# Another order in a convolution layer, halves in retention and the last norm, and unread products in three gaps

## The reference

```python
def conformer_conv_mixer(xn, ...):
    h = xn @ pw1_w + pw1_b
    a, gate = jnp.split(h, 2, axis=-1)
    h = a * jax.nn.sigmoid(gate)
    h = causal_depthwise_conv(h, dw_w, taps=31) + dw_b   # per feature, over the tokens
    h = layer_norm(h, ln_w, ln_b)                        # over the 1024 features
    return jax.nn.silu(h) @ pw2_w + pw2_b

def retention_mixer(xn, ...):                            # 4 heads
    q, k, v, g = split(xn @ w_in)                        # 1024, 1024, 2048, 2048 wide
    q, k = rotary(rms_norm(q)), rotary(rms_norm(k)) * dk ** -0.5
    y = group_norm(retention_chunkwise(q, k, v))
    return (jax.nn.silu(g) * y) @ w_out

out = rms_norm(x, g_final)                               # the very last step
```

## Time and profile before

| what | value |
|---|---|
| median of 3 runs | 2360.89 us (2360.59 to 2361.51) |
| the profiled execution | 2362.6 us |
| its span, first to last instruction | 2360.8 us |
| PE busy | 2311.3 us (98%) |
| DVE, ACT, POOL busy | 67%, 51%, 4% of the span |
| mean granted TensorE clock | 0.996 |

### The profile page before, as it was taken

The page is one execution under the profiler, slowest core; times in us unless marked ns, Lnnn a source line. Parts: engine busy times, 40 slices in busy tenths (PEclk is TensorE's granted clock), DMA queues, the critical chain, the costliest instruction groups (busy, mean ns, idle before and its releaser), DMA issues.

```text
span 2360.8 us, 31036 instructions
## 1 busy us (share of the span) xinstructions
PE 2311.3 (98%) x12362; PEld 1933.3 (82%) x12362; DVE 1571.2 (67%) x1650; ACT 1211.9 (51%) x1347; POOL 86.1 (4%) x136
## 2 busy tenths in 40 slices
PE   8999999889999999999999999999999999999998
PEld 6788888678888788877788877888888887888887
DVE  7666676766567765686576567867655667677555
ACT  5545445354356644464454365544644656446444
POOL 0000030200000000000000000000000000000000
PEclk9999999999999999999999999999999999999999
DMA  7454654634443355545454544445454544454543
GB/s 272 185 173 178 246 201 191 203 112 188 187 179 155 139 199 213 196 161 191 183 201 178 189 176 176 168 161 200 180 196 178 216 178 173 161 192 182 197 174 128
DMA packets 71848, 434.21 MB, mean 184 GB/s; under 512 B 11648, under 2 KB 11968, under 8 KB 26176
## 3 DMA queue, kind: packets, MB, share of 16 engines
q1 hardware_dynamic: 59184, 399.78, 44.2%
q0 software_dynamic: 12560, 32.96, 4.5%
HBM read 430.73 MB, written 6.16 MB: 185 GB/s over the span
## 4 chain that ended last, share of the span: by engine, by line
PE 93%; DVE 4%; ACT 2%; issue 1%; DMA 0%; POOL 0%; DVEq 0%; ACTq 0%
PE pair L807 21%; PE pair L810 11%; PE acc L778 10%; PE acc L779 10%; PE acc L780 10%; PE pair L778 6%; PE pair L780 5%; PE pair L779 5%; PE pair L819 4%; PE pair L820 2%; PE pair L1029 1%; DVE work L2304 1%; DVE w_lo L1926 1%; PE pair L848 1%; PE acc L1206 1%
## 5 line engine op out<-in xcount | busy, mean ns | idle before, releaser
L1926 DVE TENSOR_TENSOR w_lo<-raw,w_hi 128x2048 fp32r<-128x2048 f32 (+1 forms) x402 | 865.0, 2173 | 112.4 <-ACT w_hi L1327 108.6
L1327 ACT ACTIVATE w_hi<-raw 128x2048 fp32r<-128x2048 f32 (+1 forms) x402 | 717.0, 1805 | 53.7 <-PE acc L780 47.9
L807 PE MATMUL pair<-act,w_hi 128*128 128x512 f32 x1920 | 602.7, 395 | 0.0
L810 PEld LDWEIGHTS pair<-act,w_lo 128*128 128x128 f32 x1920 | 360.6, 188 | 84.8
L810 PE MATMUL pair<-act,w_lo 128*128 128x256 f32 x1920 | 377.3, 278 | 0.0
L778 PE MATMUL acc<-w_hi,hid 128*128 128x512 f32 x848 | 333.9, 394 | 0.0
L779 PE MATMUL acc<-w_lo,hid 128*128 128x512 f32 x848 | 330.4, 390 | 0.0
L780 PE MATMUL acc<-w_hi,hid 128*128 128x512 f32 x848 | 330.2, 389 | 0.0
L807 PEld LDWEIGHTS pair<-act,w_hi 128*128 128x128 f32 x1920 | 295.5, 189 | 3.6
L1472 ACT ACTIVATE gate<-pair 128x512 f32<-128x512 f32 x104 | 62.2, 598 | 458.2 <-PE pair L810 435.8
L2116 DVE TENSOR_TENSOR gate<-pair,gate 128x512 f32<-128x512 f32 x104 | 71.7, 690 | 255.0 <-ACT gate L1472 254.6
(11 more groups left out here) (273 smaller groups left out, 2671.9 us busy)
## 6 DMA issues: line engine op xcount, KB each, us to landing
raw<-weights SPq DMA_DIRECT2D x354, 1024.0 KB, 6.7
raw<-weights SPq DMA_DIRECT2D x52, 512.0 KB, 4.0
work<-bias_scratch POOLq DMA_DIRECT2D x32, 192.0 KB, 2.7
val<-gains POOLq DMA_DIRECT2D x11, 512.0 KB, 4.0
bias_scratch<-bias_rows POOLq DMA_DIRECT2D x4, 1024.0 KB, 19.9
hid<-u_rows POOLq DMA_DIRECT2D x20, 142.0 KB, 3.4
work<-ret_gn_w POOLq DMA_DIRECT2D x8, 256.0 KB, 5.3
work<-ret_gn_b POOLq DMA_DIRECT2D x8, 256.0 KB, 5.8
```

The lines of the kernel that those rows point to most:

```text
L807: mm(tiles(o[:, 512 * n:512 * n + 512]), h[:, k, n * P:(n + 1) * P], both[:, :, k, :], start=k == 0, stop=False)
L810: last = mm(o[:, 512 * n:512 * n + SEQ], l[:, k, n * P:(n + 1) * P], both[:, 0, k, :], start=False, stop=k == KT - 1)
L1327: run(w_hi[slot][:, part], raw[slot][:, part], ACT.Copy).then_inc(hi_done, 1)
L1926: tt(w_lo[slot][:, part], raw[slot][:, part], w_hi[slot][:, part].bitcast(F32), ALU.subtract).then_inc(lo_done, 1)
```

## The change

1. **Conformer, DVE's order.** `gated(1)` moves from tap 14 to tap 6, the split of unit 35 from tap 15 to 9, `gated(2)` from 27 to 14, `gated(3)` from behind the loop to tap 28 and without the split of unit 36, which comes after the loop.
2. **Conformer, the rough mean.** It is taken from tiles 2 and 3 (PE's) and no longer from tiles 0 and 1 (DVE's). PE convolves tiles 2, 3, 4, then makes the rough mean, then tiles 5, 6, 7. ACT copies tiles 2 to 4 out of PSUM with their bias; DVE takes the rough mean off tiles 0 to 4 in one instruction (128x1280) and ACT squares these five in one. The last products become four from six: tile 6 is added on DVE. `C_DSQ` is made before `C_DELTA`. POOL waits for a pair to be read, and no longer for a square, before it overwrites a place `C_X`.
3. **Retention by halves.** PE signals `token_half` after tokens 0 to 127 of a q, k or v unit; ACT copies (and squares) that half then, and the other at the unit's end. The roots come before `rotate_evac`.
4. **The last norm by halves.** DVE scales columns 0 to 511, ACT columns 512 to 1023, and SP stores four blocks of 128x512; POOL stores nothing.
5. **Unread products.** `keep_busy` issues float32 matmuls of 128x128 by 128 columns whose result nobody reads: 18 on zeroes before anything has been loaded, 12 after the first turned half at the start, 24 before unit 36 in the Conformer layer.

```diff
+            def keep_busy(m, n):
+                for _ in range(n):
+                    mm(IDLE, m, m, start=True, stop=True)
...
+            pe.wait_ge(warm_in, 1)
+            keep_busy(WARM, 18)
             pe.wait_ge(loaded, 16)
             first_half()
+            keep_busy(ident[:], 12)
...
                 unit_f()
                 unit_f()
-                pe.wait_ge(conv_ready, 2)
+                uses = [convolve(n) for n in range(3)]
+                assert uses[0] == CONV_PAIR
+                await_drained(uses[1])
                 o = open_pair()
-                for k in range(2):
-                    last = mm(o[:, 0:SEQ], C_MEAN, C_Y[:, k, :], start=k == 0, stop=k == 1)
+                for k in (2, 3):
+                    last = mm(o[:, 0:SEQ], C_MEAN, C_Y[:, k, :], start=k == 2, stop=k == 3)
                 last.then_inc(pair_full, 1)
-                uses = [convolve(n) for n in range(len(STACKED_TILES))]
+                uses += [convolve(n) for n in range(3, 6)]
                 o = open_pair()
                 pe.wait_ge(summed, 1)
...
-                for k in (6, 7):
-                    await_drained(uses[k - 2])
...
+                await_drained(uses[5])
+                mm(o[:, 0:SEQ], C_MEAN, C_Y[:, 7, :], start=False, stop=True).then_inc(mean_ready, 1)
+                pe.wait_ge(squared, 4)
+                mm(o[:, 512:512 + SEQ], C_MEAN, C_SQ[:, 7, :], start=False, stop=True).then_inc(pair_full, 1)
+                keep_busy(ident[:], 24)
...
                         if n >= 4:
-                            pool.wait_ge(squared, n - 2)
+                            p = CONV_PAIR + n - 4
+                            pool.wait_ge(drained[p % 2], p // 2 + 1)
...
-                convolve(0, 1, {4: second_piece, 14: lambda: gated(1), 15: lambda: ahead(CONV_FIRST + 3),
-                                27: lambda: gated(2)})
-                gated(3)
-                use(False)
+                convolve(0, 1, {4: second_piece, 6: lambda: gated(1), 9: lambda: ahead(CONV_FIRST + 3),
+                                14: lambda: gated(2), 28: lambda: gated(3)})
+                ahead(CONV_FIRST + 4)
+                for _ in range(4):
+                    use(False)
+                await_drained(S.p - 2)
                 await_drained(S.p - 1)
...
+                five_y = C_Y[:, 0:5, :]
+                tt(five_y, five_y, C_NEG.unsqueeze(1).broadcast_to([P, 5, SEQ]), ALU.add).then_inc(centred, 1)
...
                 for i in range(4):
-                    next_unit()
+                    ahead(S.u + 1)
                     o, done, slot = use()
-                    run(xs[:, i % 2, :], o[:], ACT.Copy).then_inc(done, 1)
...
+                    for a in range(2):
+                        if a == 0:
+                            await_half()
+                            link(run(xs[:, i % 2, wide(a)], o[:, wide(a)], ACT.Copy))
+                        else:
+                            unit_end()
+                            run(xs[:, i % 2, wide(a)], o[:, wide(a)], ACT.Copy).then_inc(done, 1)
...
+                    roots(4)
                     if i:
                         rotate_evac(i - 1)
-                    roots(4)
...
+            for a in range(2):
+                for n in range(2):
+                    sp.wait_ge(out_ready[n], a + 1)
+                    sp.dma_start(out[P * a:P * (a + 1), wide(n)], xs[:, a, wide(n)]).then_inc(out_stored, 16)
```

More of the change, by code:

```diff
@@ L389, in build_program @@
         first_copied = sem("first_copied")
+        token_half = sem("token_half")
+        out_ready = [sem(f"out_ready{n}") for n in range(2)]
+        out_stored = sem("out_stored")
+        last_root = sem("last_root")
         taps_ready = sem("taps_ready")
@@ L824, in unit_both, with unit_t @@
                 S.u += 1
-            def unit_t(middle=None, quarters=None):
+            def unit_t(middle=None, quarters=None, by_half=False):
                 o = open_pair()
@@ L882, in first_unit @@
                                      k == 0, k == KT - 1)
+                        if by_half and (a, k) == (0, KT - 1):
+                            last.then_inc(token_half, 1)
                         if a == 0 and k in (turn_at, turn_at + 1):
@@ L990, in retention @@
                         v_use = S.p
-                        unit_t(quarters=last_turn if h == 0 else None)
+                        unit_t(quarters=last_turn if h == 0 else None, by_half=True)
                     if h == 0:
@@ L1550, in retention @@
[L1550 to L1553, removed]
-                                   accum_out=ss[:, g:g + 1])
+                    for a in range(2):
[5 more added lines that the diff above has]
+                            run(xs[:, i % 2, wide(a)], o[:, wide(a)], ACT.Copy).then_inc(done, 1)
+                            await_drained(S.p - 1)
+                        for g in (2 * a, 2 * a + 1):
+                            cs = slice(SEQ * g, SEQ * (g + 1))
+                            last = run(gate[:, slot, cs], xs[:, i % 2, cs], ACT.Square, scale=RET_DK ** -0.5,
+                                       accum_out=ss[:, g:g + 1])
@@ L1564, in retention @@
                             rotate_evac(3)
-                            S.u += 1
-                            act.wait_ge(piece_used, 2 * S.u)
-                        else:
-                            next_unit()
-                            o, done, _ = use()
-                        run(R_V[:, h % 2, :, :], o[:].rearrange("p (a d) -> p a d", a=2), ACT.Copy).then_inc(done, 1)
+                        unit_end()
+                        run(R_V[:, h % 2, 1, :], o[:, wide(1)], ACT.Copy).then_inc(done, 1)
@@ L1621, in conformer @@
                 gate_unit(3, o, done)
+                for k in (2, 3, 4):
+                    o, done, _ = use(False)
+                    await_pair()
+                    run(C_Y[:, k, :], o[:, 0:SEQ], ACT.Identity, bias=colv("dw_b", k)).then_inc(done, 1)
                 o, done, _ = use(False)
@@ L1626, in conformer @@
                 act.wait_ge(centred, 1)
[L1627 to L1628 removed]
+                square(0, 5)
+                for k in (5, 6, 7):
                     use(False)
@@ L1910, in _ @@
                 square(a, 1)
-                root(a).then_inc(rstd_ready, 1)
-                S.due("x_ready")
+                root(a).then_inc(last_root, 1)
+                act.wait_ge(last_root, a + 1)
+                run(xs[:, a, wide(1)], xs[:, a, wide(1)], ACT.Copy, scale=rstd[:, a:a + 1]).then_inc(out_ready[1], 1)
             assert S.u == n_units and S.split == n_units
```

84 lines of the change are left out of this document (42 added, 42 removed).

## The result

The changed kernel takes 2349.55 us (median of 5 runs, 2348.77 to 2351.76) where the kernel before takes 2361.51 in the same comparison: a ratio of 0.9946, 95% interval 0.9933 to 0.9960. Run again in a later comparison it gave 2349.47 and 0.9945 (0.9932 to 0.9959). The forecast was 2340.0 with a range of 2335.5 to 2348.0. So the sign was right, the gain is 12 to 13 us and not 21, and the time lies just outside the range. The profiled execution took 2348.81 us with a span of 2347.0, 13.8 less than before.

The account below looks back on a forecast made before the run. PE was taken as the bound, busy 2311.3 of 2360.8 us. Gains of 13.75 (Conformer), 1.5 (unit 36), 3.5 (retention), 0.8 (start) and 1.25 (end) sum to 20.8, giving 2340.0 us, range 2335.5 to 2348.

Parts of the forecast that it names:

- (d): Conformer layer, stop of 4.29 us before tile 6: goes if loads come in time; gain 4.3, and 1.6 more.
- (a): Conformer layer: split of unit 35 comes 2.4 us or more earlier, so PE's unit ends at 443.85; gain 0.85.
- (c): Conformer layer, first four stacked tiles: 13.8 us without the lower clock, 14.8 before; gain 1.0.
- (f): Conformer closing chain up to unit 36: `C_DSQ` before `C_DELTA` starts the root some 0.3 us earlier; gain 0.15.
- Rival 1: Conformer layer, u_rows transfers still come late; 2344 to 2348, or about 2353 at worst; chance 0.17.
- middle case: Late u_rows transfers in the Conformer layer: a stop of 3 to 6 us at one tile and the clock; 2344 to 2348.
- (b): Conformer layer: tile 2 starts at the unit's end, rough mean after tile 4 at full rate, 0.9 us; gain 4.9.
- (e): Conformer closing sums: four products, no tile 6 sum at the end; 0.86 us to the same product, 1.8 before; gain 0.95.
- rival 3: DVE is the bound in the Conformer closing stage, 2 to 4 us later than counted: 2341 to 2343; chance 0.10.
- 24 unread products: Before unit 36: 5.2 us in the idle stretch, unit 36 then at full rate; net gain 1.5, bounds 0 and 2.9.
- The start: Unread products (18 and 12) around PE's first turn bring full rate earlier; gain 0.8, bounds -1.7 and 1.0.
- The end: Last norm: earlier scaling 0.35, no POOL issue delay 0.3, smaller last block 0.6; gain 1.25, bounds 0.5 and 2.

Follow-up runs that it names:

- experiment 1: Changed kernel with SP holding unit 38's load until the shifted copies of tile 7 have landed: 2342.8 us, ratio 0.9915.
- experiment 6: Changed kernel without the three calls of `keep_busy`, so without any of the 54 unread products: 2350.79 us, ratio 0.9948.

## Why the forecast missed

**The step that failed is (d).** It said that the third store and its loads run "when SP has no weight transfer in flight". Three things in it were off. First, its own rebuild had the split of unit 36 end at 454.1 and the eight loads be issued up to 455.4 and land by 459; the split's end is what lets SP load unit 38, so that load stood in the text at 454.1, in the middle of the loads. Shown: with that one load held, the stop is 1.19 and not 6.00 us (experiment 1). Second, the split of unit 35 was costed as DVE's work that comes earlier, (a), and its effect on SP only against the second store, as "5 us at 426 GB/s, done by 438". It shares the engines with eight loads of 142 KB, and the DMA engines stay busy until about 442. So the second set starts at 443.91 and POOL, which goes through its program in order, can only issue the third store at 448.27, 3 us later than forecast once the 2.0 of the earlier layers is taken off. Third, the usual landing of 3.5 us was taken from stores and loads that lay clear of the weights, while the same row's 9.9 was the price for those that don't.

What it cost: unit 36 was forecast at 473.6, 471.6 once the 2.0 us of the earlier layers are taken off, and came at 481.25. Of these 9.7 us, 7.1 are the two stops and 1.8 the clock behind the longer one; of the remaining 0.8 most is in the tiles (2 to 5 take 14.4 us without the stop, where (c) had 13.8), and 0.1 or 0.2 each in the rough mean, tiles 6 and 7, and the sums ahead of tile 7's. The closing chain held: from tile 7's product at 474.02 to unit 36 it is 7.23 us, 7.38 before, as (f) had it. With unit 38's load held the layer gives 10.0 of the 13.75 (four profiles of the old order have 85.4 on average to unit 36, this one 75.4), and 2.6 of what is then missing are its two stops.

**Rival 1 is what happened**, with 0.17 of the chances. Its middle case was a stop of 3 to 6 us; there were 6.0 and 1.06, and the time came out 1.6 us above what that case gave.

**The other steps.** (a) and (b) held: tile 2 starts at 441.75, forecast 443.85 less 2.0, and the rough mean took 1.13 and not 0.9. (c) held as to the clock: it is granted in full at tile 4, in spite of the stop ahead of it. (e) held: two products, 0.97 us, lie ahead of tile 7's, where I had counted 0.86. DVE was not the bound (rival 3): it waits 8.84 us for tile 6. Of the 24 unread products the duration was right, 5.52 us for 48 instructions is 0.23 for a product (forecast 0.215); the gain, forecast at 1.5, is 1.4 by one pair of profiles and 2.2 over all, within the bounds. Retention was forecast from the list of waits at 3.5; both layers gave 4.3, within the bounds; the 0.8 beyond the waits I haven't traced.

**The start** was forecast at 0.8; the ledger's 0.1 is the luck of one execution, and over all profiles it gave about 1 (experiment 6), so nothing shows that this step failed. The profile on which the forecast rests has its second turned half at 17.20, where the other five without products have it at 17.86 to 18.48. The overrun of 18 products was larger than "up to 1 us" in the changed kernel: the first turn starts at 8.04 for 6.79, but at 7.04 when the same program ran again. The prediction took 3.1 and 5.8 us as agreement with a half rate that differs from run to run at a start; those were two stops of one execution, and only the starts of several profiles, listed below, show it.

**The end** was forecast at 1.25 and gave 2.9. The term that was mis-sized is POOL's tail. I had counted the delay of its issue and the bytes; what follows the last byte, 2.8 us for POOL and 0.85 for SP, was in the row of the span's end and I hadn't read it. That is 2.0 of the 2.6 us from the last scaling on. The kernel with only this part ends 0.85 us after its last bytes too (moved until 2355.65, span 2356.5), and the one with only retention, which keeps POOL's store, 2.8 (2354.2, 2357.0). The Trainium skill, DMA: Bandwidth & Descriptors (Anatomy of one DMA — SWDGE (gpsimd) path), puts most of some 2 us of fixed cost of GpSimd's path behind the last byte. The profile agrees in kind: in the layer, too, the DMA engines have all but fallen idle at 442.5 (a share of 0.05 from there to 443), and POOL, which waits for the second store, goes on at 443.91. Of SP's path no figure stands there. Of the same page's first byte after 0.6 us (Specifications) the measurement is 0.86, from the issue at 2343.91 to the first bytes at about 2344.77.

**What stays open.** The best kernel here is the changed one with unit 38's load held, 2342.8 us, 6.8 below the changed kernel where both ran side by side (2349.47 and 2342.67, with 12 products). It still has stops of 1.43 and 1.19, since the second store is waited for 10.35 us. An order in which units 37 and 38 both miss all of POOL's transfers wasn't found: the three places tried for unit 37 each met one of them. Why the parts' product is 0.0012 below the whole I can't say; the intervals allow for nothing at all.

## What to carry to other kernels

A split or a buffer release that moves earlier takes its refill (the load into the buffer that it frees) with it: write down for each queue when its transfers are now in flight, and lay them beside all others in order of time, before any of them is given its usual landing. A transfer of 142 or 287 KB that met a 2 MB load took 7 to 10 us here and not 3 to 4; making the big load wait was worth 6.8 us, and here a load that had slack was better held than hurried. Follow PE past the stop that is taken away to the next engine's work: at the start 2.4 us between PE's first products were 0.4 one unit later. And read a gain of 1 us in more than one pair of profiles: two single executions put the start at 0.1 and unit 36 at 1.4, and fourteen put them at about 1 and at 2.2.

## What the runs showed of the hardware

- DMA engines can be fully busy at half their rate: share 0.98 to 1.02 at 209 to 247 GB/s with stacked copies of a tile, 410 with weights.
- The kernel ends 2.8 us after the last bytes of its last store when POOL issues it, and 0.85 us after them when SP does (two profiles each). For a store in the layer the engines had been all but idle for 1.4 us when POOL went on.
- How long the half rate lasts differs between executions of the same program. The 18 products on zeroes took 7.13 us in the changed kernel and 6.05 when it ran again; in four more kernels with the same start they took 5.76, 6.24, 6.95 and 7.13. Behind unit 36 the granted clock rose after 5.8 us in one profile and 3.7 in another. In the changed kernel's windows from 1 to 7 us the granted clock nevertheless stands at 1.00, while 9 to 12 instructions pass in 2 us and 20 do at 8 to 10 us: there the count tells the rate, and the column doesn't. The Trainium skill, TensorE: Matmul & The Clock Gate, part 1, says that the number at the low rate at a start varies from run to run, which these six agree with.
